# Narrow norms, an opening by blocks of tokens, and other places for loads and squares

## The reference

```
def rms(x, g):
    x32 = x.astype(jnp.float32)
    y = x32 * lax.rsqrt(jnp.mean(x32 * x32, axis=-1, keepdims=True) + EPS)
    return (y * g.astype(jnp.float32)).astype(x.dtype)

# first block
h = rms_norm(x, g_norm);  z = h @ w_in          # 8716 columns: q k v f gf u gs qm gm and three gates
merged = gates[0] * (y_fox @ w_proj_fox) + gates[1] * (y_s5 @ w_proj_s5) + gates[2] * (y_mem @ w_proj_mem)
x = rms_norm(x + merged @ w_out, g_final)
# second block, layers l = 0, 1
ada = silu(c) @ w_ada[l] + b_ada[l];  sh1, sc1, gt1, sh2, sc2, gt2 = split(ada, 6)
h = rms(x, g_mix[l]) * (1.0 + sc1) + sh1
parts = h @ w_in[l]
...
x = x + gt1 * (mixed @ w_out[l])
h2 = rms(x, g_mlp[l]) * (1.0 + sc2) + sh2
x = x + gt2 * (square(relu(h2 @ w_ff1[l])) @ w_ff2[l])
```

## Time and profile before

| | us |
|---|---|
| median of 3 runs | 2602.92 (2602.31 to 2603.13) |
| the profiled execution | 2601.7 |
| its span, first to last instruction | 2599.7 |
| TensorE busy | 2384.8 (92%) |
| VectorE busy | 1454.2 (56%) |
| GpSimd busy | 1126.4 (43%) |
| ScalarE busy | 597.2 (23%) |
| mean granted TensorE clock | 0.964 |

### The profile page before, as it was taken

The page is one execution under the profiler, slowest core; times in us unless marked ns, Lnnn a source line. Parts: engine busy times, 40 slices in busy tenths (PEclk is TensorE's granted clock), DMA queues, the critical chain, the costliest instruction groups (busy, mean ns, idle before and its releaser), DMA issues.

```text
span 2599.7 us, 30892 instructions
## 1 busy us (share of the span) xinstructions
PE 2384.8 (92%) x12709; PEld 1889.6 (73%) x12709; DVE 1454.2 (56%) x1756; ACT 597.2 (23%) x1212; POOL 1126.4 (43%) x672
## 2 busy tenths in 40 slices
PE   5798868799999969999998999998999999899998
PEld 3677835677666639977756888886997766688887
DVE  3799444424333667455458857747645537764341
ACT  2133325313222221134402334201114430100000
POOL 3543223143333525642124666663662305466663
PEclk8899978899999989999999999998999999999999
DMA  5334660341444432221032665533231104233321
GB/s 163 114 77 111 182 235 1 122 146 61 133 146 148 157 96 99 97 78 48 18 107 72 202 192 177 178 109 103 89 98 61 34 17 146 65 98 98 97 97 49
DMA packets 274280, 280.87 MB, mean 108 GB/s; under 512 B 29580, under 2 KB 256080, under 8 KB 274012
## 3 DMA queue, kind: packets, MB, share of 16 engines
q1 hardware_dynamic: 242012, 243.97, 29.6%
q10 hardware_dynamic: 32128, 34.92, 4.4%
HBM read 257.87 MB, written 17.85 MB: 106 GB/s over the span
## 4 chain that ended last, share of the span: by engine, by line
PE 68%; DVE 5%; ACT 1%; issue 1%; ACTq 0%; DVEq 0%
PE ps L433 43%; PE ps L1858 11%; PE ps L525 6%; PE ps L757 2%; PE ps L800 2%; PE ps L776 1%; DVE ps L864 1%; DVE normed L651 1%; DVE hT_low L641 1%; PE ps L786 1%; DVE root L646 1%; PE ps L627 1%; PE ps L1954 1%; PE ps L358 0%; DVE squares_summed L585 0%
## 5 line engine op out<-in xcount | busy, mean ns | idle before, releaser
L226 POOL TENSOR_SCALAR ring_high<-ring 128x1024 fp32r<-128x1024 f32 x302 | 335.1, 1110 | 1347.7 <-DMA ring<-in_w_in_dram 360.9
L228 POOL TENSOR_TENSOR ring_low<-ring,ring_high 128x1024 fp32r<-128x1024 f32 x302 | 762.2, 2524 | 25.2
L433 PE MATMUL ps<-hT_high,ring_high 128*128 128x512 f32 x816 | 329.1, 403 | 19.1 <-DVE hT_low L641 5.8
L433 PE MATMUL ps<-hT_low,ring_high 128*128 128x512 f32 x816 | 319.3, 391 | 0.0
L433 PE MATMUL ps<-hT_high,ring_low 128*128 128x512 f32 x816 | 319.2, 391 | 0.0
L345 DVE TENSOR_REDUCE ada_acc<-ring 128x256 f32<-128x2048 f32 x48 | 188.8, 3934 | 111.4 <-ACT ring L332 111.1
L1858 PE MATMUL ps<-ring_high,hT_high 128*128 128x256 f32 x768 | 221.8, 289 | 10.4 <-DVE hT_low L641 10.4
L1858 PE MATMUL ps<-ring_high,hT_low 128*128 128x256 f32 x768 | 219.6, 286 | 0.0
L1858 PE MATMUL ps<-ring_low,hT_high 128*128 128x256 f32 x768 | 219.5, 286 | 0.0
L332 ACT ACTIVATE ring<-ring,c_act 128x256 f32<-128x256 f32 x384 | 158.5, 498 | 186.2 <-DMA ring<-in_w_ada_dram 186.1
L433 PE MATMUL ps<-hidden_high,ring_high 128*128 128x512 f32 x512 | 200.0, 391 | 0.0
(11 more groups left out here) (341 smaller groups left out, 4164.1 us busy)
## 6 DMA issues: line engine op xcount, KB each, us to landing
ring<-in_w_in_dram SPq DMA_DIRECT2D x75, 1024.0 KB, 5.3
ring<-in_w_ff_dram SPq DMA_DIRECT2D x64, 1024.0 KB, 5.5
ring<-in_w_ada_dram SPq DMA_DIRECT2D x48, 1024.0 KB, 7.3
ring<-in_w_out_dram SPq DMA_DIRECT2D x12, 1024.0 KB, 6.6
scratch_x<-xT ACTq DMA_DIRECT2D x3, 2048.0 KB, 7.5
xT<-scratch_x ACTq DMA_DIRECT2D x3, 2048.0 KB, 8.6
ring<-in_w_mem_kv_dram SPq DMA_DIRECT2D x4, 1024.0 KB, 5.5
ring<-in_w_branch_a_dram SPq DMA_DIRECT2D x8, 512.0 KB, 6.1
```

The source lines that it names most:

```text
L226: nc.gpsimd.tensor_scalar(hi, raw, 1.0, 1.0, ALU.mult, ALU.mult).then_inc(hi_done.sem, 1)
L228: nc.gpsimd.tensor_tensor(lo, raw, hi.bitcast(F32), ALU.subtract).then_inc(lo_done.sem, 1)
L433: ins = nc.tensor.matmul(out[0:rows, bank, cols[0]:cols[1]], lhsT, rhs, start=start, stop=stop)
```

## The change

Six parts:

1. **The opening.** x is loaded in four blocks of tokens with a semaphore each. ScalarE squares each block along its rows with an accumulated sum (128x1024 to one column), so the sum of squares lies with tokens on partitions; the root and the reciprocal are 128x4. VectorE multiplies the identity by the reciprocals (`diagonals`, 128x512), and one product with ones spreads them over all partitions. Evictions of `xT` are shared by VectorE and ScalarE, the parameters' rows are transposed in between, and the norm's gain, high and low parts follow in the same stage. The nine S5 parameter loads move from ScalarE's queue to the sync engine's, ahead of the fourth weight slab, behind waits for x's transposes and squares. The silu of c and the halved biases now come behind this norm.
2. **Narrow norms** (`norm_stage`) at the layers' norms. TensorE multiplies the summed squares, as the stationary operand, by one column of ones, four 1-column products, and then the last tile's square in the same way, which is thus no longer added on VectorE. Root and reciprocal are 128x4, then the diagonal and the spread as above. A small root is issued ahead so that its table is loaded.
3. **The two norms between the blocks become one** (`twice`). The out stage's squares move to ScalarE, a plain one and one times `g_final`, and VectorE keeps two sums; in the norm both are turned to columns and the second norm's root is worked out from both. x itself is written (eight operations of VectorE) behind the norm's output.
4. **Two tiles per arrival.** With `arriving`, `tiles_stage`, `Stream.feed` and the second block's first slab (tiles 0 and 2, then 1 and 3) feed two tiles for each k-tile that arrives.
5. **ada's slabs.** The out stage's four move to the merge stage, one between gate and projection slab of each group's first branch.
6. **The rope tables** are loaded ahead of the out stage, and for the second layer behind the first layer's second norm.

```
@@ plan_slabs
             add(f"merge{mp}{b}g", w, dm, O_GL + D * b, D, part=mp)
+            if b == 0:
+                ada(0)
             add(f"merge{mp}{b}p", T[pw][0], (0, rows), 0, D, False, part=mp)
             ada(0)
-    add_ada("out", T["w_out"][0], dm, 0, D, 0)
+    add("out", T["w_out"][0], dm, 0, D)
@@ tiles_stage, TensorE
+                for j in range(0, size, per):
+                    pe.wait_ge(arriving[0].sem, arriving[1] + max(j // per + 1, arriving[3]))
+                    for n in range(2):
+                        for x in range(j, j + per):
+                            ins = product(n, x)
@@ add_square
+    if n == KD - 1:
+        return ins
@@ norm_stage (new), TensorE, one norm
+                for t in range(TT):
+                    ins = nc.tensor.matmul(ps[:, bank + t, 0:1], x[:, t * P:(t + 1) * P], K.ones[:, 0:1],
+                                           start=not last, stop=last)
...
+            pe.wait_ge(diagonal.sem, d0 + 1)
+            nc.tensor.matmul(ps[:, 7, :], K.ones, diag[:, 0], start=True, stop=True).then_inc(spread.sem, 1)
@@ norm_stage, VectorE
+                step(v.reciprocal(nar[:, 4, :], nar[:, 3, :]))
+            diagonals(0, nar[:, 4, :]).then_inc(diagonal.sem, 1)
@@ s5_stages
-    arriving = rms_stage(K, K.xT, SEQ, K.g_norm, K.hT)
+    def load_parameters(sp):
+        sp.wait_ge(K.sig("x_turned").sem, KD)
+        sp.wait_ge(K.sig("x_squared").sem, TT)
+        sp.dma_start(lamn[:, 0, 0:P5], T["lam_re"][0]).then_inc(loaded.sem, 16)
...
+    K.sync_turns[K.first["u"] + SLOTS] = [load_parameters]
@@ load_stage, ScalarE
+            for t in range(TT):
+                e.wait_ge(xl[t].sem, 16)
+                if t:
+                    e.wait_ge(squared.sem, t)
+                nc.scalar.activation(squares[:, :], xn[:, t, :], ACT.Square, accum_out=nar[:, 0, t:t + 1]
+                                     ).then_inc(squared.sem, 1)
+            e.wait_ge(squared.sem, TT)
+            nc.scalar.activation(nar[:, 3, :], nar[:, 0, :], ACT.Sqrt, bias=K.eps[:, 0:1], scale=1.0 / D
...
@@ block_one, out stage, VectorE and ScalarE
+        if 2 <= n:
+            e.wait_ge(squared.sem, 2 * n)
+            for x in range(2):
+                a = square[:, 0, x, :] if n == 2 else sums[x]
+                ins = v.tensor_tensor(sums[x], a, square[:, (n - 1) % 2, x, :], ALU.add)
+            ins.then_inc(summed.sem, 1)
...
+        nc.scalar.activation(square[:, n % 2, 0, :], xq[:, n, :], ACT.Square).then_inc(squared.sem, 1)
+        nc.scalar.activation(square[:, n % 2, 1, :], xq[:, n, :], ACT.Square, scale=K.g_final[:, n:n + 1]
...
@@ layer
+    arriving = norm_stage(K, K.xT, gains[:, 1, :], K.hT, ada[:, 24:32], K.sums, K.square_last)
+    if l + 1 < LAYERS:
+        rope_loads(K, T, l + 1)
```

More of the change, by code:

```diff
@@ L397, in tiles_stage @@
             ada.setdefault(max(n - 2, 0), []).append(K.ada_after[key])
+    for slabs in ada.values():
+        slabs.sort()
     if ada and dve is None:
@@ L413, in _, with product @@
             seen = set()
+            def product(n, j):
+                bank, rows, cols, lhsT, rhs, key, start, stop = tiles[n][j]
+                out = view(n)
+                if key is not None and key not in seen:
+                    seen.add(key)
+                    K.weight_here(pe, key)
+                if rhs is None:
+                    return nc.tensor.transpose(out[0:rows, bank, cols:cols + lhsT.shape[0]], lhsT,
+                                               K.ident[0:lhsT.shape[0], 0:lhsT.shape[0]])
+                return nc.tensor.matmul(out[0:rows, bank, cols[0]:cols[1]], lhsT, rhs, start=start, stop=stop)
+            first = 0
+            if arriving is not None:
+                first = 2
+                size = len(tiles[0])
+                per = 1 if tiles[0][0][5][1] is None else 3
+                for j in range(0, size, per):
[3 more added lines that the diff above has]
+                            ins = product(n, x)
+                        if j + per == size:
+                            ins.then_inc(made.sem, 1)
             for n, t in enumerate(tiles):
+                if n < first:
+                    continue
                 if n >= bufs:
@@ L438, in _ @@
                 ada_sum(K, pe, s)
-        if act is None and ada:
+        if act is None and (ada or also is not None):
             @block.scalar
@@ L603, in rms_stage @@
     with K.stage() as block:
-        KS = 1 if summed else KD
         @block.scalar
         def _(e):
-            for k in range(0 if summed else KD):
+            for k in range(KD):
                 if k >= 2:
@@ L1553, in load_stage @@
+    ld.total += 16 * (2 + len(vec))
+    cl.total += 16
+    for g in (*xl, ):
+        g.total += 16
+    for g in (eps, root, diagonal, spread, rows_turned, cols):
+        g.total += 1
+    for g in (squared, by_dve, by_act):
+        g.total += 4
+    for g in (turned, scaled, high, low):
+        g.total += KD
+    K.close(loads=ld, tensor=spread, xdve=by_dve, xact=by_act, cols=cols)
+    arriving = (low, 0, dict(K.last), 1)
+    K.close(scalar=high, vector=low)
     ha, si = K.sig("biases_halved"), K.sig("c_activated")
```

434 lines of the change are left out of this document (318 added, 116 removed).

## The result

The changed kernel takes 2571.97 us, the median of 4 runs (2570.75 to 2576.6), where the kernel before takes 2602.61 in the same comparison. The ratio is 0.9884, with a 95% interval of 0.9871 to 0.9898. It is 31 us faster; 63 were forecast, and 2571.97 lies above the range.

What follows compares the result with a forecast made beforehand. TensorE's products plus the stretches in which it has nothing to multiply bound the kernel; gains 28.5 - 13.4 + 3.3 + 24.3 + 0 + 9.9 + 11.1 = 63.7 led to 2539.2 us, range 2521 to 2560.

Steps and rivals of the forecast that it cites:

- The single norms and two tiles per arrival: Layers' three single norms: first product 6.3 earlier, both tiles end with the last arrival; second layer gains 9.9 and 11.1.
- T: The end of TensorE's last product before a norm, from which the forecast counts times in us.
- The merge stage: Between the blocks: ada slabs moved here delay projection slabs, and TensorE waits for their take and sums; cost 13.4.
- rival (d): First layer's feed-forward: the ring never catches up, cycle 15.8 where two tiles take 10.9; 118 lost, 2657; chance 0.04.
- rival (a): Merges: both ada slabs are hidden, as a projection slab issued behind one overlaps it; 13 faster, 2526; chance 0.14.
- 3.0 per MB: Merge stage: load time in us per MB, used to put the projection slab 2.0 late behind an ada slab.
- The opening: Start of the kernel: low halves end at 17.4 to 32.7, parameters' copy at 34.3 instead of 61.79; gain 28.5.
- rival (c): Opening: the parameters land after 40 instead of by 27, and the branch starts there; 10 lost, 2549; chance 0.09.
- The out stage: Before the double norm: without its four ada slabs the stage takes 43.6 instead of 47.0; gain 3.3.
- The double norm: Between the blocks: two norms become one, first four token tiles done at T + 33.5 instead of 57.8; gain 24.3.
- Rival (b): Thin work in shorter gaps lets TensorE's clock fall, slowing arrivals at four places by 20, partly hidden; 2555; chance 0.15.
- The first feed-forward: First layer: the norm is shorter but the ring is late, TensorE resuming at T + 41; gain 0, from -2 to +5.

Runs made afterwards that it cites:

- e2: The changed kernel with the shared region's base not rounded up to 64 bytes, 32 bytes lower, at the same residue as the split weights; 2563.4 us.
- e4: The kernel before with 160 unused bytes behind the gains, putting every buffer where the changed kernel has it; 2614.56 us, ratio 1.0043.
- e7: e2 with 20 instead of 3 unused 384-column products on TensorE in the opening; 2566.27 us.
- e6: e2 with the nine issues for the second layer's rope tables moved to the 13th tile of the first layer's feed-forward; 2562.92 us.
- e11: e2 with the first of the merge stage's four ada slabs moved behind the first slab of the memory's keys; 2548.59 us.

## Why the prediction was wrong

**The single norms and two tiles per arrival: right.** The first product was put at T + 8.2. In the last stage of e2 it came at T + 8.19 (2188.34 to 2196.53), and the stage gained 10.8 for the forecast 11.1; the second mix gained 10.0 for 9.9. In the changed kernel the same two stages gained 4.1 and 8.7. The last stage holds 768 of the slower products, 5.1 us; the rest is the clock, which was granted 0.66 in the ten us of that norm (2191 to 2201; 1.00 in those of e2), so that the spread and the products behind it came at half speed:

```profile
2195.63 2.08 PE L758 MATMUL ps<-diagonals,const 128*128 128x512 f32 x2 [0.60 <-DVE diagonals L796]
...
2200.77 0.81 PE L429 MATMUL ps<-hT_high,ring_high 128*128 128x512 f32 x1
```

against the earlier trace rows, where the first product took 0.47. **One step that failed is one that I never wrote**: every product of TensorE was taken to cost what it cost before. An edit that adds small buffers moves all others, and 2112 products took 0.0066 longer, some 14 us by themselves and 10.4 in e4.

**The merge stage: mechanism right, size wrong for the first group. This is the step that cost most: 31.2 for 13.4.** The sum had 2.0 for the projection three times, 1.5 for the take and 0.35 for the sum four times. Groups 1 to 3 lost 3.6 to 5.4 each, together 13.2 (11.6 by those terms). What failed is the clause in brackets, that the first group is loaded early, by which its projection was put at no cost. It is, but being loaded early is what hurts it: the first ada slab sits in the ring from 586.82 on, the second from 599.17, and nobody scales them until the first tile is done, so the next gate slab, not the projection, comes late. That is rival (d)'s cycle in another place, and it cost 18.0 with the clock. My bound of 25 for the whole was passed by 6, and rival (a), that the merges hide the slabs, fell. (In the working of the 3.0 per MB, 0.75 MB is what stands ahead of the ada slab and 2.75 includes the gate slab itself. The two are 1 MB apart, so the rate stands.)

**The opening: right within 5.** The low halves were put at 17.4 to 32.7, and they ended at 16.4 to 30.4, in steps of 2.05 and 0.74, in turn with GpSimd. What I missed is on the weights' side. GpSimd's timeline in the changed kernel, then TensorE's:

```profile
15.76 1.50 POOL L226 TENSOR_SCALAR ring_high<-ring 128x1024 fp32r<-128x1024 f32 x1 [15.32 <-DMA ring<-in_w_in_dram]
17.35 2.66 POOL L228 TENSOR_TENSOR ring_low<-ring,ring_high 128x1024 fp32r<-128x1024 f32 x1
```

```profile
20.15 0.76 PE L550 MATMUL ps<-hT_high,ring_high 128*128 128x512 f32 x1 [4.14 <-POOL ring_low L228]
...
24.26 0.80 PE L550 MATMUL ps<-hT_high,ring_high 128*128 128x512 f32 x1 [2.49 <-POOL ring_low L228]
```

Two tiles per arrival need both halves of the first slab. The second half was split at 24.2, and until then TensorE had one product group to do; its clock fell to 0.50 in 22 to 26 us. The copy came at 37.86 instead of 34.3. How early the first slab lands is not fixed by the code: in the eleven executions with this opening (all but e7) GpSimd began it between 13.72 and 16.15 and the copy came between 33.87 (e2, slab at 13.72) and 37.86. Their mean is 35.9, so the forecast is 1.6 off on the average, and most of the 4.6 is scatter in a load that the sum had no term for. The parameters' loads were hidden, so rival (c) fell.

**The out stage: 0.6 for 3.3.** I priced 192 products at 0.227 and left out that the stage begins at half clock, as it did before (0.83 in the first 10 us of both); 1.3 more are the addresses.

**The double norm: 23.8 for 24.3**, T + 14.2 for T + 16.8 to the first product. Rival (b), the clock, came true at this place in nine of ten executions; it cost 3.3 of the gain in e2 (20.5), and with the 1.4 in the last norm of the changed kernel it stays far below the 16 that it had for four places. VectorE's eight operations behind the norm cost nothing that the trace shows. The sentence on the drain did not hold here: the first operation behind the table load started 0.02 us after it (934.16 + 1.28, then 935.46), where the Trainium skill, "ScalarE: Activation LUTs", section "What ACT_TABLE_LOAD costs", adds 1.38.

**The first feed-forward: about 0 as forecast**, by its mechanism in part: TensorE's last wait ended at T + 39.7 for the forecast T + 41. Its time went otherwise than in one wait of 10 behind the fourth tile:

```profile
1400.29 1.01 PE L360 MATMUL ps<-const,ada_acc 128*128 128x1 f32 x4 [4.28 <-DVE ada_acc L347]
...
1410.45 0.58 PE L360 MATMUL ps<-const,ada_acc 128*128 128x1 f32 x4 [1.42 <-DVE ada L370]
```

It waited 4.28 behind the third tile, made the fourth in 7.9 instead of 5.45 (the clock was at 0.50 until 1405.6), and waited 1.42 more. Behind it no wait of the stage is over 1.0, so rival (d)'s cycle did not come. The stage gained 2.7 in e2 and lost 2.7 in the changed kernel, and its 768 slower products are 5.1 of the difference. That the wait is led by the nine issues is only partly so (e6).

In sum, of the 32.5 that are missing 17.8 are the merge stage, most of it in the first group; 4.6 are the opening, within its scatter; and the other 10.1 are near the price of the addresses (10.4 between e4 and the kernel before). That last match is in part luck, since the 10.1 also hold the 4.0 of the branch and some clock.

## What to carry to other kernels

A slab that is loaded early and consumed by an engine behind the first tile holds its slot all that time. Where a ring is short, ask of each slab who frees it, where that stands in the queue, and which load waits for the slot; a place where TensorE is elsewhere and the slab can be consumed at once is free (e11, 15 us for one slab). After any edit that adds or resizes a buffer, compare the pitch of the main products in a stretch without waits; here one expression was worth 9 us. Before moving work off an engine or onto it, price it against the stage as the change leaves it, not as it was: the ada slabs were priced at 3.3 by the old out stage and cost 21 in the new one.

## What the runs showed of the hardware

- The pitch of 128x512 products of the rounded kind (fp32r) depended on the distance, within 128 bytes, between the region of the moving operand and the fixed buffers of the stationary one: 0.2267 us at 0, 0.2333 at 32, 0.229 at 64 (one execution), at the same granted clock of 1.00. Plain float32 products of the same size from that region kept their 0.429.
- An unused 384-column product of unrounded float32 took 0.65 us at full clock (20 in 13.06), where a 512-column product of the rounded kind is 0.227 behind the last.
- At the same place and after the same 2.3 us of idle TensorE, the clock stayed at its upper level until T + 8 in one execution and fell to 1.2 GHz by T + 4 in nine; between the changed kernel and e2 the norm's end differed by 4.6 us.
- With one program text for the opening, the first weight slab was ready between 13.7 and 16.2 us, and all that follows it moved with it by up to 4 us.
